# A gated linear-attention scan whose chunk products are cut from eight full blocks to thirteen narrower ones

## The reference

```python
def gla_chunk_scan(q, k, v, lg, s0):            # lg: log of the decay, per token and key channel
    def step(s, inp):
        qc, kc, vc, gc = inp
        g = jnp.cumsum(gc, axis=2)
        decay = jnp.exp(jnp.where(mask, g[:, :, :, None, :] - g[:, :, None, :, :], -jnp.inf))
        att = jnp.einsum('bhik,bhjk,bhijk->bhij', qc, kc, decay)
        o = einsum(att, vc) + einsum(qc * jnp.exp(g), s)
        s = s * jnp.exp(g_last) + einsum(kc * jnp.exp(g_last - g), vc)
        return s, o
# lg = log_sigmoid((h @ w_g1[d]) @ w_g2[d] + b_g[d]) / 16, d = 0 forwards, 1 backwards; four heads;
# the outputs of both directions are added. Key width 128, value width 256 per head.
```

## Time and profile before

| | |
|---|---|
| runs of the kernel before | 3654.77, 3656.49 (median), 3658.05 us |
| the profiled execution: its own time, its span | 3655.85 us, 3653.7 us |
| VectorE busy over the whole span | 65% |
| stretch 700 to 800 us, inside the scan: VectorE, TensorE, GpSimd, ScalarE busy | 99%, 86%, 52%, 39% |
| granted TensorE clock in that stretch, in parts of its full speed | 1.00 |

### The profile page before, as it was taken

One profiled execution on the slowest core, in us unless ns is written; L12 is line 12 of the kernel. 1 busy time (PEld: TensorE's weight loads), 2 busy tenths in 40 slices (PEclk: granted clock), 3 DMA queues, 4 the chain that ended last, 5 costly groups with the idle time before them and its releaser, 6 DMA issues. The chain is left out here.

```text
span 3653.7 us, 48736 instructions
## 1 busy us (share of the span) xinstructions
PE 3303.3 (90%) x17622; PEld 2787.3 (76%) x17622; DVE 2391.6 (65%) x2972; ACT 974.5 (27%) x1352; POOL 1019.3 (28%) x539
## 2 busy tenths in 40 slices
PE   5989988887889999999998668988898899999998
PEld 3889877776768888888887547777777678888886
DVE  7975099999645666666666436656664556666666
ACT  4111233333332111111111424444443221111111
POOL 1323155554222222222221131112111333333331
PEclk8999999999889999999999879999999999999999
DMA  5557210000411111111110200000002111111111
GB/s 203 184 190 262 79 47 1 0 0 16 141 41 41 35 40 40 36 38 34 35 45 0 78 8 10 5 5 5 5 2 81 47 50 42 52 52 46 46 46 58
DMA packets 64155, 196.38 MB, mean 54 GB/s; under 512 B 7665, under 2 KB 20849, under 8 KB 62641
## 3 DMA queue, kind: packets, MB, share of 16 engines
q1 hardware_dynamic: 47200, 164.36, 13.3%
q10 hardware_dynamic: 16848, 30.56, 2.4%
HBM read 176.02 MB, written 18.87 MB: 53 GB/s over the span
## 5 line engine op out<-in xcount | busy, mean ns | idle before, releaser
L1379 DVE SCALAR_TENSOR_TENSOR resid<-ps,mod,resid 128x512 f32<-128x512 f32 (+1 forms) x880 | 601.9, 697 | 472.3 <-PE ps L1275 472.0
L1282 PE MATMUL ps<-hf_hi,up_hi 128*128 128x512 f32 (+1 forms) x1760 | 652.9, 371 | 31.1 <-DVE hf_lo L283 22.1
L1282 PE MATMUL ps<-hf_lo,up_hi 128*128 128x512 f32 (+1 forms) x1760 | 652.0, 370 | 0.0
L1282 PE MATMUL ps<-hf_hi,up_lo 128*128 128x512 f32 (+1 forms) x1760 | 650.1, 369 | 0.0
L1250 POOL TENSOR_SCALAR up_hi<-up_raw 128x1024 fp32r<-128x1024 f32 x88 | 94.5, 1073 | 1160.8 <-PE ps L1282 1100.0
L1282 PEld LDWEIGHTS ps<-hf_hi,up_hi 128*128 128x128 f32 x1760 | 334.7, 190 | 88.3 <-issue 34.2
L1282 PEld LDWEIGHTS ps<-hf_hi,up_lo 128*128 128x128 f32 x1760 | 333.9, 190 | 56.4
L1282 PEld LDWEIGHTS ps<-hf_lo,up_hi 128*128 128x128 f32 x1760 | 334.8, 190 | 51.4
L1275 PE MATMUL ps<-act_hi,dn_hi 128*128 128x512 f32 (+1 forms) x880 | 332.9, 378 | 18.5 <-DVE act_lo L1400 16.1
L1331 ACT ACTIVATE conv<-ps,conv_w 128x1280 f32<-128x1280 f32 (+1 forms) x88 | 115.6, 1314 | 803.1 <-PE ps L1282 802.9
L1275 PE MATMUL ps<-act_lo,dn_hi 128*128 128x512 f32 (+1 forms) x880 | 326.6, 371 | 0.0
(11 more groups left out here) (237 smaller groups left out, 7009.7 us busy)
## 6 DMA issues: line engine op xcount, KB each, us to landing
up_raw<-in_up SPq DMA_DIRECT2D x88, 512.0 KB, 3.2
adaw_ring<-in_adaw SPq DMA_DIRECT2D x80, 512.0 KB, 4.0
dn_raw<-in_dn SPq DMA_DIRECT2D x44, 512.0 KB, 3.2
vr<-vr_out ACTq DMA_DIRECT2D x80, 128.0 KB, 3.4
adaw_first<-in_adaw SPq DMA_DIRECT2D x16, 512.0 KB, 22.0
wvr_raw<-in_wvr SPq DMA_DIRECT2D x8, 1024.0 KB, 6.8
x<-in_xT ACTq DMA_DIRECT2D x8, 640.0 KB, 16.7
r<-vr ACTq DMA_DIRECT2D x10, 512.0 KB, 3.8
```

Of the source, the lines that this page charges most:

```text
L1282: mm = pe.matmul(c.psf[:, at:at + w], a[:, half, k, :], b[:, k, t:t + w], start=(k == 0 and a is up_hi and b is h_hi), stop=(k == KD - 1 a ...
L1379: dve.scalar_tensor_tensor(resid[:, m, t:t + w], c.ps[:, 6 + j % 2, 0:w], c.mod[:, gate + m, cond[t]:cond[t] + 1], resid[:, m, t:t + w], A ...
```

## The change

Five things change together, all within `gla_scan` and the constants that it uses.

1. The levels of 128, 64 and 32 tokens stay, but each product is cut to the keys of one half and the queries of the other: one product of 64 x 64, two of 32 x 32 and four of 16 columns (with 16 or 32 keys, as the direction has it). They lie on top of each other in one block of 128 columns.
2. The levels of 16 and 8 tokens become one: a group of 16 is cut into four quarters, the query is scaled once (from the start of its quarter), and three key blocks (`QUARTERS`, `QUARTER2`, `QUARTER3`) serve the second, third and fourth quarter with 32 columns each. The level of 4 is one product of 64 columns; the level of 2 and the diagonal are two of 64 columns with the unscaled query. The results of a unit fill four blocks of 128 columns, one PSUM bank, and there are two such banks.
3. VectorE scales six blocks by the query instead of eight in two instructions, GpSimd nine blocks by the key instead of ten. Mask and sum are replaced by four `copy_predicated` of 128 columns, each of which waits for the one in front; `att` is cleared once.
4. ScalarE takes over `fade` and, where the output is only copied, that copy. The gate's passes work in PSUM: `Abs` on ScalarE and no pass for the negative on VectorE; the transposed key moves to another bank. `w2` is loaded again for this stage.
5. On TensorE and VectorE the steps are written out instead of looped. In `decay` the high and the low part alternate bank by bank, and the last bank waits for the copy of the transposed key.

```diff
-LEVELS = 7
-DIAG, CUM, REST = LEVELS, LEVELS + 1, LEVELS + 2
-NBLK = LEVELS + 3
+COARSE = 3
+CUM, LEVEL, QUARTERS, PAIRS, QUARTER2, QUARTER3, LAST, REST = 0, 1, 4, 5, 6, 7, 8, 9
+NBLK = 10
+NQUERY, NKEY = 6, 9
+PICKS = 4
...
             sp.dma_start(mask[:, :, :], mask_d).then_inc(mask_in, 16)
             for at, sem in ((slice(0, 2), v_first), (slice(2, NT), v_rest)):
                 sp.dma_start(v[:, at, :], vr_d[at, :, 0:D].rearrange("t p n -> p t n")).then_inc(sem, 16)
+            sp.dma_start(w2[:, :], w2_d).then_inc(w2_in, 16)
...
-                for n, a in enumerate((lg_hi, lg_lo)):
-                    for t in range(0, NBLK * P, BANK):
-                        m = min(BANK, NBLK * P - t)
+                for t in range(0, NBLK * P, BANK):
+                    m = min(BANK, NBLK * P - t)
+                    if m < BANK and (u >= 2 or not begins(s)):
+                        pe.wait_ge(kt_set, s * U + (u - 1))
+                    for n, a in enumerate((lg_hi, lg_lo)):
                         mm = pe.matmul(c.psf[:, E_PS + t:E_PS + t + m], a[:, d, h * P:(h + 1) * P],
                                        tree[:, d, t:t + m], start=(n == 0), stop=(n == 1))
...
-                pe.wait_ge(masked_set, s * U + u)
-                for b in range(LEVELS):
-                    pe.matmul(c.psf[:, TREE_PS + b * P:TREE_PS + (b + 1) * P],
-                              kd[u % 2][:, b * P:(b + 1) * P], qd[:, u % 2, b * P:(b + 1) * P],
-                              start=True, stop=True)
+                for b in range(COARSE):
+                    size = P >> b
+                    half = size // 2
+                    for k0 in range(0, P, size):
+                        left, right = (k0, k0 + half) if d == 0 else (k0 + half, k0)
+                        m = half
+                        if left % 32:
+                            left, m = k0, size
+                        q0 = (LEVEL + b) * P + right
+                        pe.matmul(c.psf[left:left + m, at + right:at + right + half],
+                                  keys(LEVEL + b)[:, left:left + m],
+                                  qd[:, u % 4, q0:q0 + half], start=True, stop=True)
+                own = qd[:, u % 4, QUARTERS * P:(QUARTERS + 1) * P]
+                for n, block in ((1, QUARTERS), (2, QUARTER2), (3, QUARTER3)):
+                    level(1, keys(block), own, 16, 4, n)
+                level(2, keys(PAIRS), qd[:, u % 4, PAIRS * P:(PAIRS + 1) * P], 4, 2, 1)
+                level(3, keys(LAST), query[:, 0, :], 2, 2, 1)
+                level(3, key[:, 0, :], query[:, 0, :], 2, 2, 0).then_inc(tree_done, 1)
...
-                dve.tensor_tensor(masked[:, :], c.psf[:, TREE_PS:TREE_PS + LB], mask[:, d, :],
-                                  ALU.mult).then_inc(masked_set, 1)
-                dve.wait_ge(masked_set, s * U + (u + 1))
-                dve.wait_ge(o_done, s * U + (u + 1))
-                dve.tensor_reduce(att[:, u % 2, :], masked[:, :].rearrange("p (b t) -> p t b", t=P),
-                                  AX.X, ALU.add).then_inc(att_set, 1)
+                for n in range(PICKS):
+                    if n == 0:
+                        dve.wait_ge(tree_done, s * U + (u + 1))
+                    dve.wait_ge(picked, (s * U + u) * PICKS + n)
+                    mm = dve.copy_predicated(
+                        att[:, d, u % 2, :], mask[:, d, n * P:(n + 1) * P].bitcast(mybir.dt.int32),
+                        c.psf[:, at + n * P:at + (n + 1) * P])
+                    mm.then_inc(picked, 1)
...
-                if fresh:
-                    dve.tensor_copy(oc, c.psf[:, O_PS:O_PS + GDV].unsqueeze(1)).then_inc(o_added, 1)
-                else:
+                if not fresh:
```

More of the change, by code:

```diff
@@ L736, in _, with gla_scan @@
                                   ALU.subtract).then_inc(lg_split, 1)
-def gla_scan(c, qk, v, o, g1, gates, mask_d, vr_d):
+def gla_scan(c, qk, v, o, g1, gates, mask_d, w2_d, vr_d):
     nc, U = c.nc, 2 * GH
[L752 to L763, removed]
-    fade = c.at("fade", 19.75, [P, 4])
[L765 to L771, removed]
@@ new lines, in gla_scan @@
+    tree, g1s, lg_hi, lg_lo = gates.tree, gates.g1s, gates.lg_hi, gates.lg_lo
+    mask = c.at("mask", 151, [P, 2, PICKS * P])
+    state = c.at("state", 157, [P, U, GDV])
+    e = c.at("decay", 165, [P, 2, NBLK * P])
+    w2 = c.at("w2", 175, [64, GH * GDK])
+    decayed_log = c.at("gate_log", 177, [P, GH * GDK])
+    att = c.at("att", 205, [P, 2, 2, P])
+    kt = c.at("k_turned", 179, [P, 2, P])
+    qd = c.at("q_decayed", 189, [P, 4, NQUERY * P])
+    kd = [c.at("k_decayed0", 208, [P, NKEY * P]), c.at("k_decayed1", 218, [P, NKEY * P])]
@@ L837, in products @@
                 d, h = divmod(u, GH)
+                raw = slice(h, h + 1), slice(GH + h, GH + h + 1)
+                query, key = (qk[:, at, bass.ds(chunk[d] * P, P)] for at in raw)
                 pe.wait_ge(q_set, s * U + (u + 1))
                 pe.wait_ge(k_set, s * U + (u + 1))
-                pe.wait_ge(masked_set, s * U + u)
-                for b in range(LEVELS):
-                    pe.matmul(c.psf[:, TREE_PS + b * P:TREE_PS + (b + 1) * P],
-                              kd[u % 2][:, b * P:(b + 1) * P], qd[:, u % 2, b * P:(b + 1) * P],
-                              start=True, stop=True)
@@ new lines, in level @@
+                def level(pick, key, query, size, parts, n):
+                    n = n if d == 0 else parts - 1 - n
+                    to = c.psf[:, at + pick * P:at + (pick + 1) * P]
+                    return pe.matmul(part(to, size, parts, n), key, part(query, size, parts, n),
+                                     start=True, stop=True)
+                for b in range(COARSE):
[10 more added lines that the diff above has]
+                                  qd[:, u % 4, q0:q0 + half], start=True, stop=True)
@@ L852, in products @@
-                pe.transpose(c.psf[:, GATE_PS:GATE_PS + P], kd[u % 2][:, REST * P:NBLK * P],
+                pe.wait_ge(e_set, s * U + (u + (1 if ends(s) and u == U - 1 else 2)))
+                pe.transpose(c.psf[:, TURN_PS:TURN_PS + P], kd[u % 2][:, (REST - LEVEL) * P:NKEY * P],
                              c.ident[:, :]).then_inc(turned, 1)
@@ L949, in body @@
                         decay(s + 1, u + 2 - U)
+                    if u and fresh:
+                        keep_output(s, u - 1, chunk)
+                    elif not u and prev_fresh:
+                        keep_output(s + (-1), U - 1, prev)
                     if nxt and u in (1, 5):
@@ L997, in query_state @@
[L997 to L1004 removed]
+                    qd[:, u % 4, :].rearrange("p (b t) -> p b t", t=P),
@@ L1441, in gla_layer @@
     o = c.at("o", 111, [P, NT, D])
-    gla_scan(c, qk, v, o, g1, gates, a["mask"], a["vr"])
+    gla_scan(c, qk, v, o, g1, gates, a["mask"], a["w2"], a["vr"])
     y_hi = c.at("y_hi", 21, [P, KD, T], F32R)
```

178 lines of the change are left out of this document (95 added, 83 removed).

## The result

The changed kernel takes 3598.11 us (3595.76 to 3599.71, four runs) against 3657.27 beside it: a ratio of 0.984, 95% interval 0.983 to 0.985, 59 us less where 31 less were forecast. The profiled execution has a span of 3594.8 us, against 3653.7.

The account below looks back on a forecast made before the run. VectorE bounds at 5.54 us a unit, TensorE next: 2.28 + 1.17 + 0.12 + 1.29 + 0.31 = 5.17. So 3655.85 - 29 - 2 = 3625 us, own range 3605 to 3645, 8 in 10 3585 to 3675.

Parts of the forecast that it names:

- the price of the twelve narrow passes: TensorE's coarse products with 32 and 16 weight columns: 0.030 us a pass, part of 0.47 us for all fourteen.
- rival (a): TensorE's narrow passes nearly free, no wait at shape changes: 4.82 us a unit, 3597; paired passes 3583; chance 0.25.
- The changes of shape: TensorE empties when weight width changes, three times a unit: 0.27 us plus exposed loads, 0.35 us.
- the gate: Its products on TensorE add 1.26 us, twice in eight units, 0.31 a unit; two shape changes at 0.20 each.
- Wide passes: TensorE passes with 128 weight columns, not cheaper with fewer moving columns: thirteen at 0.112, 1.46 us a unit.
- The sums: Sums of logs on TensorE, after the products: 1.17 us a unit.
- The demand of TensorE before: TensorE's unit without waits in the old kernel: 4.25 us, 4.56 with the gate, of 5.54.
- VectorE's work: VectorE's sum for a unit after the change: 2.97 us against 5.54, up to 3.5 at the dear end.
- rival (c): Query and GpSimd collide on VectorE in every unit: 2.97 + 2.6 = 5.57 us, 3656, no gain; chance 0.13.
- Rival (b): TensorE empties at every move to another tile position: 5.77 us a unit, 16 us slower, 3672; chance 0.17.
- The last bank: The sums' last bank newly waits for the transposed key's copy of 0.28 us, with 0.3 us to spare.
- The chances: Faster 0.72, same 0.12, slower 0.16; the forecast itself had 0.45.

Follow-up runs that it names:

- the first experiment: Changed kernel with the product of the level of 128 cut into two of 32 keys by 64 queries: 3592.59 us, ratio 0.983.

## Why the prediction came out as it did

The direction and its reason held: VectorE was relieved, TensorE became the engine without gaps, and its demand set the new unit. The forecast size was about half of what came: 4.82 us a unit instead of 5.17, 0.35 x 79 = 28 us, which is the whole of the difference between 59 and 31. The time lies below the forecast's own range (3605 to 3645) and inside the range for 8 in 10.

- **The step that failed is the price of the twelve narrow passes.** "I take 0.057 for the two and 0.030 for the twelve": by loads that start 0.009 us apart the twelve take 0.11 us, not 0.36. That is 0.25 of the 0.35. The estimate was right for passes on one tile (0.028) and left out that the seven products lie on different tiles. The possibility stood in rival (a), as a further 0.18, and was not put into the forecast because no row showed it.
- **The changes of shape cost what was said.** 0.35 us for three was taken from the gate. One more costs 0.13, one fewer saves 0.13 with two passes added. Rival (a)'s time, 3597, is close to what came, but not for its reason: the changes are not free, the passes are.
- **Wide passes.** The thirteen come at (708.34 - 707.05) / 12 = 0.1075 us instead of 0.112, 0.06 a unit. Narrow moving sides gain that little and no more. The sums (708.45 to 709.61, 1.16) and the gate (1.25) came as forecast. Of the remaining 0.04, 0.03 is that 18 gates in 80 units make 0.28 on average and not 0.31; the rest is rounding.
- **The room.** The demand of TensorE before, 4.56, counted 0.22 for a weight load beside the last output; the kernel with wide coarse levels, whose unit of 4.53 without a gate has two passes more than before (nineteen, not seventeen), gives 4.53 - 0.22 + 0.31 = 4.62. This did not enter the forecast of after, where that load stands open. It also says that the new products raised TensorE's demand, from about 4.62 to 4.82.
- **VectorE.** The copies cost 1.30 in a unit against 1.24. VectorE's work is 2.97 by the prediction without a collision; with the queries of 2.16 on average it is 4.3 of 4.82, and the 89% busy stand against the 55 to 65% that were forecast.
- **The collision, rival (c).** It happens in most units and holds nothing up: the query of the unit that starts at 711.11 is ready at 708.88, 2.2 us early, where the prediction had 1.8. In about half of the units the margin is smaller, as in the next one: the query ends at 712.98 + 1.72 = 714.70 and the products start at 715.66, 0.96 later. The products wait for the query in two units only, the first and the last of the scan, 1.8 us together. In the kernel with half a mask it did cost, since VectorE had no room there.
- **Rival (b), a drain at each move of tile, is refuted:** moving makes passes cheaper (0.009 against 0.028).
- **The last bank.** The transposed key's copy ends at 709.04 and the loads of the sums follow without a gap, as predicted; the two banks for the products, which the prediction gave no price, are worth 6 to 10 us.
- **The chances.** "Faster" at 0.72 is more than the 0.25 and 0.45 that it was said to be made of.

The Trainium skill's page "TensorEngine Tiling (Array Packing)", section "Key Properties", has both halves: a change of mode drains, different tiles run in parallel. I used the first and left the second to a rival. The runs show both, with 0.13 us and 0.009 against 0.028.

What carried the gain, then, is the lighter VectorE: it made room down to TensorE's demand, and that demand did not fall but rose by 0.2 us a unit. The new cut of the products paid because four copies can pick up its results. The narrowing of the coarse levels, with three changes of shape, gave nothing over three plain wide products (3596 against 3598). Kept to one shape, narrow products give 80 us more. No run shows how VectorE's relief divides among the four copies, the shorter query and the work that went to ScalarE. The steps written out instead of looped were not tried by themselves either; VectorE, which set the pace, was busy 99.4% with its loop, so they can have given little there.

## What to carry to other kernels

Where a product uses only small blocks, cut all products of the stage into tiles of one shape and order them so that neighbours lie on different tiles; here a mix of shapes paid 0.13 us at each change, and that ate the whole gain of the narrowing. Price an instruction in the company it runs in: a pass was three times cheaper (0.009 for 0.028), a small VectorE product five times dearer (1.58 for 0.29), by what ran beside it. When the bound is lifted from one engine, work out the next engine's pace row by row, and look for what the freed engine now runs into.

## What the runs showed of the hardware that was not expected

- Passes with 32- and 16-column weights, neighbouring products on different tiles, start 0.009 us apart over twelve, 0.010 over sixty-four and 0.014 over the sixteen of the first experiment, loads of 0.1 us each lying side by side; on one tile 0.028.
- Passes with 128-column weights take 0.1075 us on average with 32 and 64 moving columns, hardly less than the 0.111 with 128.
- A product of two SBUF inputs on VectorE that started inside GpSimd's product ended after it: a small one 0.14 us behind it, so that 0.29 us became 1.58, and a query 0.8 behind it (708.88 against 708.08). The queries of after range from 0.96 to 3.39.
- A predicated copy of 128 columns from PSUM takes 0.298 us on average.
